# Eight of eleven up-projection iterations as seven block products of half-length matmuls, in a float32 decoder trunk on one Trainium2 core

## The reference, cut to what matters

```python
D_FF = ((8 * D_MODEL // 3 + 127) // 128) * 128        # 2816
def conv_ffn(x, norm_g, w_up, conv_w, conv_b, w_down):
    h = rms_norm(x, norm_g)
    a, b = jnp.split(h @ w_up, 2, axis=-1)
    a = lax.conv_general_dilated(a, conv_w[:, None, :], window_strides=(1,),
                                 padding=[(CONV_WIDTH - 1, 0)], ...
                                 feature_group_count=D_FF) + conv_b
    return (jax.nn.silu(a) * b) @ w_down
```

## Time and profile before

| | |
|---|---|
| median of 3 runs | 1625.05 us (1625.04 to 1625.46) |
| profiled execution | span 1624.1 us, 0.95 us less than the median |
| PE busy | 1617.6 us |
| DVE, ACT, POOL busy | 971.4, 670.6, 109.9 us |
| granted TensorE clock | 1.00 over the whole span |
| DMA | 154.59 MB, mean 95 GB/s |

### The profile page before, as it was taken

The page is one execution under the profiler, slowest core; times in us unless marked ns, Lnnn a source line. Parts: engine busy times, 40 slices in busy tenths (PEclk is TensorE's granted clock), DMA queues, the critical chain, the costliest instruction groups (busy, mean ns, idle before and its releaser), DMA issues.

```text
span 1624.1 us, 19782 instructions
## 1 busy us (share of the span) xinstructions
PE 1617.6 (100%) x7482; PEld 1348.9 (83%) x7482; DVE 971.4 (60%) x1167; ACT 670.6 (41%) x807; POOL 109.9 (7%) x157
## 2 busy tenths in 40 slices
PE   9999999999999999999999999999999999999998
PEld 7888888888888888888888888888888888888887
DVE  7267875775666666533362778657756666556222
ACT  5244335532345445522233543345333554454213
POOL 4000000000310000002020000000004000000020
PEclk9999999999999999999999999999999999999999
DMA  5332222223232323323233322222233322232322
GB/s 189 104 117 78 78 78 91 79 68 101 91 99 95 97 97 92 102 92 102 91 116 96 112 78 78 78 91 76 77 94 99 96 93 101 91 103 90 111 91 91
DMA packets 44701, 154.59 MB, mean 95 GB/s; under 512 B 4960, under 2 KB 5472, under 8 KB 44640
## 3 DMA queue, kind: packets, MB, share of 16 engines
q1 hardware_dynamic: 42480, 148.86, 28.0%
q10 hardware_dynamic: 2160, 4.86, 1.1%
HBM read 149.50 MB, written 2.10 MB: 93 GB/s over the span
## 4 chain that ended last, share of the span: by engine, by line
PE 99%; DMA 0%; DVE 0%; ACT 0%; issue 0%; SPq 0%; DVEq 0%; ACTq 0%
PE ps L1045 30%; PE ps L1043 30%; PE ps L1044 30%; PE ps L1051 2%; PE ps L1050 2%; PE ps L1049 2%; PE ps L1172 1%; PE ps L1161 1%; PE ps L1139 1%; PE ps L1143 1%; PE ps L1295 0%; PE ps L1183 0%; DMA xs<-xt 0%; PE ps L1109 0%; PE ps L1180 0%; PE ps L1340 0%
## 5 line engine op out<-in xcount | busy, mean ns | idle before, releaser
L1043 PE MATMUL ps<-u_hi,w_hi 128*128 128x512 f32 x1344 | 525.5, 391 | 0.0
L682 DVE TENSOR_TENSOR w_lo<-w_raw,w_hi 128x1024 fp32r<-128x1024 f32 x274 | 350.6, 1289 | 291.8 <-ACT w_hi L431 287.7
L1045 PE MATMUL ps<-u_hi,w_lo 128*128 128x512 f32 x1344 | 523.3, 389 | 0.0
L1044 PE MATMUL ps<-u_lo,w_hi 128*128 128x512 f32 x1344 | 523.2, 389 | 0.0
L431 ACT ACTIVATE w_hi<-w_raw 128x1024 fp32r<-128x1024 f32 x274 | 286.6, 1055 | 278.7 <-DMA w_raw<-wts 272.0
L1045 PEld LDWEIGHTS ps<-u_hi,w_lo 128*128 128x128 f32 x1344 | 252.3, 188 | 53.0
L1044 PEld LDWEIGHTS ps<-u_lo,w_hi 128*128 128x128 f32 x1344 | 252.5, 188 | 50.9
L1043 PEld LDWEIGHTS ps<-u_hi,w_hi 128*128 128x128 f32 x1344 | 252.5, 188 | 50.5
L1045 PE MATMUL ps<-g_hi,w_lo 128*128 128x512 f32 x264 | 102.7, 389 | 0.0
L1043 PE MATMUL ps<-g_hi,w_hi 128*128 128x512 f32 x264 | 102.7, 389 | 0.0
L1044 PE MATMUL ps<-g_lo,w_hi 128*128 128x512 f32 x264 | 102.7, 389 | 0.0
(11 more groups left out here) (211 smaller groups left out, 2190.1 us busy)
## 6 DMA issues: line engine op xcount, KB each, us to landing
w_raw<-wts SPq DMA_DIRECT2D x274, 512.0 KB, 3.5
q<-q ACTq DMA_DIRECT2D x8, 256.0 KB, 3.5
xs<-xt SPq DMA_DIRECT2D x7, 256.0 KB, 6.6
out<-rows SPq DMA_DIRECT2D x7, 256.0 KB, 2.5
dec<-decay ACTq DMA_DIRECT2D x2, 514.0 KB, 4.1
w_raw<-wts SPq DMA_DIRECT2D x4, 256.0 KB, 6.2
cs<-rope ACTq DMA_DIRECT2D x2, 512.0 KB, 3.6
lastg<-last ACTq DMA_DIRECT2D x1, 256.0 KB, 4.3
```

The costliest lines, as they stand in the source:

```text
L682: nc.vector.tensor_tensor(w_lo[:, s, :], w_raw[:, s, :], w_hi[:, s, :].bitcast(F32), ALU.subtract).then_inc(s_lo, 1)
L1043: nc.tensor.matmul(dst, a_hi, b_hi, start=start, stop=False)
L1044: nc.tensor.matmul(dst, a_hi, b_lo, start=False, stop=False)
L1045: return nc.tensor.matmul(dst, a_lo, b_hi, start=False, stop=stop)
```

## The change

Of the 11 up iterations of a layer the first three (`PLAIN`) stay as they are. The other eight (`SPLIT`) treat an iteration, which is a product of 512 x 1024 by 1024 x 512, as a 2 x 2 block product: tokens in an early and a late half, k in two halves, output channels in the `a` and the `b` half. Its four weight quarters are W11, W21 (both k halves of `a`), W12, W22 (of `b`). Eight block products would make it in the plain way; here seven are made, over sums of quarters and sums of activation blocks, and the four output blocks are put together from them.

* **Weights.** Seven parts of 128 x 1024 for each iteration: part 0 = W11, 1 = W11 + W12, 2 = W22 + part 1, 3 = W21, 4 = W12 + W22, 5 = W22, 6 = W21 + part 2. SP loads seven quarters (`load_split`). The second summand of parts 1 and 4 comes in by a DMA that POOL issues and that adds to what lies there (`add_parts`); parts 2 and 6 are added up by DVE (`third_sum`, `fourth_sum`). Then ACT and DVE split each part (`part_high`, `part_low`).
* **Activations**, once a layer: ACT applies the norm's gain (`with_gain`), POOL multiplies four and adds four blocks of 128 x 1024 (`combine`), and ACT and DVE split the seven results (`comb_high`, `comb_low`), the first three after the second plain iteration, the other four after the third.
* **PE.** A product has 2 x 4 x 3 = 24 matmuls of 128 x 256. Three banks are used. Products are accumulated on one another, and ACT copies intermediate sums out between them (`copy_x`, `copy_y`, `copy_u`), for which PE waits.
* **Outputs.** DVE makes three of the four blocks (2 x 256 per partition) from PSUM and a copy, ACT the last one. The convolution of iteration n runs during iteration n + 1; the gate product of a split iteration moves to POOL (`gated`) and stays unsplit in `g_raw`.
* **Down.** The seven activation sums lie where `g_hi` is to be. So the split of the gated tiles (`gated_high`, `gated_low`, two tiles at a time) is moved behind the products: pair 0 in the last split iteration, pair s + 1 during down slab s, on each engine behind the split of weight slab s + 3.

```diff
-DOWN0 = UP0 + 2 * FT
+PLAIN = 3
+PAIRS = FT // 2
+SPLIT = PAIRS - PLAIN
+DOWN0 = UP0 + 4 * PLAIN
...
+            def load_split(l):
+
+                base = l * SLABS + DOWN0 - RING + SLOT_CREDIT
+                sp.wait_ge(s_free, base + 1)
+                load_part(l, 0, 0, W11, s_el[0])
+                sp.wait_ge(s_free, base + 2)
+                load_part(l, 0, 1, W11, s_el[1])
+                sp.wait_ge(s_free, base + 3)
+                load_part(l, 0, 2, W22, s_el[2])
+                load_part(l, 0, 6, W21, s_el6[0])
+                sp.wait_ge(s_free, base + 4)
+                load_part(l, 0, 3, W21, s_el[3])
+                load_part(l, 0, 4, W12, s_el[4])
+                load_part(l, 0, 5, W22, s_el[5])
+                for n in range(SPLIT):
+                    done = 7 * (l * SPLIT + n)
+                    more = n + 1 < SPLIT
+                    if more:
+                        if n > 0:
+                            sp.wait_ge(s_prod, done)
+                        load_part(l, n + 1, 6, W21, s_el6[(n + 1) % 2])
+                    sp.wait_ge(s_prod, done + 1)
+                    if more:
+                        load_part(l, n + 1, 0, W11, s_el[0])
+                    else:
+                        load(ring(l, 0), l * SLABS + DOWN0)
...
+            def combine(l):
...
+                nc.gpsimd.tensor_tensor(a22[:], a22[:], late, ALU.mult).then_inc(s_v, 1)
+                nc.gpsimd.tensor_tensor(late2[:], late2[:], late, ALU.mult).then_inc(s_v, 1)
...
+            def add_parts(l, n, k):
+
+                landed, added, which = (s_el[1], s_sum1, W12) if k == 1 else (s_el[4], s_sum3, W22)
+                pool.wait_ge(landed, 16 * (l * SPLIT + n + 1))
+                nc.gpsimd.dma_start(part_raw(l, n, k), wts[DEPTH * SLABS + (l * SPLIT + n) * 4 + which, :, :],
+                                    accum_op=ALU.add).then_inc(added, 16)
...
+            def gated_high(l, c):
+
+                act.wait_ge(s_gf, l * FT + 2 * c + 2)
+                last = 7 * SPLIT * (l + 1)
+                act.wait_ge(s_prod, last - 6 if c < 2 else last)
+                nc.scalar.activation(g_hi[:, 2 * c:2 * c + 2, :], g_raw[:, 2 * c:2 * c + 2, :], ACT.Copy).then_inc(s_ghh, 1)
...
+                    if g == PLAIN - 1:
+                        for k in range(3, 7):
+                            comb_high(l, k)
+                for n in range(SPLIT):
...
+                    part_high(l, n, 3)
+                    act.wait_ge(s_prod, done + 1)
+                    if n > 0:
+                        act.wait_ge(s_c11, l * SPLIT + n)
+                    nc.scalar.activation(copy_x[:], half_tiles(banks(n)[0]), ACT.Copy).then_inc(s_cpx, 1)
+                    part_high(l, n, 4)
...
+                    act.wait_ge(s_prod, done + 2)
...
+                    nc.scalar.activation(copy_u[:], half_tiles(banks(n)[0]), ACT.Copy).then_inc(s_cpu, 1)
+                    part_high(l, n, 6)
+                    for k in range(3):
...
+                        else:
+                            split_hi(l, DOWN0 + k)
+                            if k == 1:
+                                gated_high(l, 0)
...
                 for i in range(DOWN0, SLABS):
...
                     if i + AHEAD < SLABS:
                         split_hi(l, i + AHEAD)
+                    if i - DOWN0 + 1 < PAIRS:
+                        gated_high(l, i - DOWN0 + 1)
...
+            def third_sum(l, n):
+
+                m = l * SPLIT + n
+                dve.wait_ge(s_sum1, 16 * (m + 1))
+                dve.wait_ge(s_el[2], 16 * (m + 1))
+                nc.vector.tensor_tensor(part_raw(l, n, 2), part_raw(l, n, 2), part_raw(l, n, 1), ALU.add).then_inc(s_sum2, 1)
+
+            def fourth_sum(l, n):
+
+                m = l * SPLIT + n
+                dve.wait_ge(s_sum2, m + 1)
+                dve.wait_ge(s_el6[n % 2], 16 * (l * (SPLIT // 2) + n // 2 + 1))
...
+            def gated_low(l, c):
+
+                dve.wait_ge(s_ghh, l * PAIRS + c + 1)
+                nc.vector.tensor_tensor(g_lo[:, 2 * c:2 * c + 2, :], g_raw[:, 2 * c:2 * c + 2, :], g_hi[:, 2 * c:2 * c + 2, :].bitcast(F32),
+                                        ALU.subtract).then_inc(s_gl, 2)
...
+                        elif i + AHEAD == DOWN0 + 2:
+                            third_sum(l, 0)
+                            fourth_sum(l, 0)
+                            part_low(l, 0, 1)
...
+                    dve.wait_ge(s_prod, 7 * m + 5)
+                    dve.wait_ge(s_cpy, m + 1)
+                    dve.wait_ge(s_gf, l * FT + 2 * (PLAIN + n))
+                    nc.vector.tensor_tensor(cb[:, :, S // 2:S], half_tiles(a), copy_y[:], ALU.subtract).then_inc(s_c22, 1)
+                    if n + 1 < SPLIT:
+                        third_sum(l, n + 1)
+                    else:
+                        split_lo(l, DOWN0 + 1)
+                        gated_low(l, 0)
+                    dve.wait_ge(s_prod, 7 * m + 6)
+                    dve.wait_ge(s_cpu, m + 1)
+                    nc.vector.tensor_tensor(cb[:, :, 0:S // 2], copy_u[:], half_tiles(c), ALU.subtract).then_inc(s_tile, 4)
+                    if n + 1 < SPLIT:
...
                     if i + AHEAD < SLABS:
                         split_lo(l, i + AHEAD)
+                    if i - DOWN0 + 1 < PAIRS:
+                        gated_low(l, i - DOWN0 + 1)
...
+                def product(n, k, bank, fresh, ends):
+
+                    hi, lo = part_hi(l, k), part_lo(l, n, k)
+                    pe.wait_ge(s_elo, 7 * (l * SPLIT + n) + k + 1)
+                    if n == 0:
+                        pe.wait_ge(s_combl, l * 7 + k + 1)
+                    for t in range(2):
+                        for kk in range(4):
+                            o = kk * 256 + t * P
+                            mm = three_open(ps[:, bank, t * 256:t * 256 + 256], hi[:, o:o + P], lo[:, o:o + P],
+                                            comb_hi[k][:, kk, :], comb_lo[k][:, kk, :], fresh and t == 0 and kk == 0, ends and kk == 3)
+                    mm.then_inc(s_prod, 1)
...
+                    product(n, 0, a, True, False)
+                    product(n, 1, c, True, False)
+                    pe.wait_ge(s_cpx, m + 1)
+                    product(n, 2, a, False, False)
+                    product(n, 3, b, True, True)
+                    pe.wait_ge(s_cpu, m + 1)
+                    product(n, 4, a, False, False)
+                    pe.wait_ge(s_cpy, m + 1)
+                    product(n, 5, c, False, True)
+                    pe.wait_ge(s_c22, m + 1)
+                    product(n, 6, a, False, True)
 
```

More of the change, by code:

```diff
@@ L305, in trunk @@
         s_gl = sem("s_gl")
+        s_v = sem("s_v")
+        s_xgain = sem("s_xgain")
+        s_comb = sem("s_comb")
+        s_combh = sem("s_combh")
+        s_combl = sem("s_combl")
+        s_el = [sem(f"s_el{k}") for k in range(6)]
+        s_el6 = [sem(f"s_el6{b}") for b in range(2)]
+        s_sum1 = sem("s_sum1")
+        s_sum3 = sem("s_sum3")
+        s_sum2 = sem("s_sum2")
+        s_sum4 = sem("s_sum4")
+        s_eh = sem("s_eh")
+        s_elo = sem("s_elo")
+        s_prod = sem("s_prod")
+        s_cpx = sem("s_cpx")
+        s_cpy = sem("s_cpy")
+        s_cpu = sem("s_cpu")
+        s_c11 = sem("s_c11")
+        s_c21 = sem("s_c21")
+        s_c22 = sem("s_c22")
+        s_ghh = sem("s_ghh")
         s_xga = sem("s_xga")
@@ L347, in _, with load_one, load_ring @@
             assert DEPTH * SLABS % RING == 0
-            with sp.Fori(1, DEPTH * SLABS // RING) as r:
-                for j in range(RING):
-                    sp.wait_ge(s_free, r * RING + j + 1)
-                    load(j, r * RING + j)
+            def load_one(n):
+                sp.wait_ge(s_free, n + 1)
+                load(n % RING, n)
+            def load_ring(first, end):
+                a, b = -(-first // RING), end // RING
+                for n in range(first, a * RING):
+                    load_one(n)
+                with sp.Fori(a, b) as r:
+                    for j in range(RING):
+                        sp.wait_ge(s_free, r * RING + j + 1)
+                        load(j, r * RING + j)
+                for n in range(b * RING, end):
+                    load_one(n)
@@ new lines, in plain_tap, with silu @@
+            def plain_tap(l, g, h):
+                f = 2 * g + h
+                act.wait_ge(s_tile, l * TILES + TILE_CREDIT + UP_TILE + 2 * f + 1)
+                if f >= 2:
+                    act.wait_ge(s_gf, l * FT + f - 1)
+                nc.scalar.activation(cc[:, h, :], ca[:, h, 2:2 + S], ACT.Identity, scale=taps(l, f, 2), bias=taps(l, f, 3)).then_inc(s_c1, 1)
+            def silu(l, f):
+                act.wait_ge(s_cv, l * 2 * FT + 2 * f + 2)
+                nc.scalar.activation(cc[:, f % 2, :], cc[:, f % 2, :], ACT.Silu).then_inc(s_c2, 1)
@@ L609, in _ @@
                 root(l, 1)
[L610 removed]
+                for g in range(PLAIN):
                     for j in range(4):
```

(22 more changed lines are left out.)

344 lines of the change are left out of this document (290 added, 54 removed).

## The result

The changed kernel takes **1650.46 us** (median of 4 runs, 1648.33 to 1652.25) against 1625.05 us for the kernel before (4 runs, 1624.83 to 1625.46). The ratio is 1.0155, 95% interval 1.0141 to 1.0169: 25.4 us slower. The profiled execution has a span of 1650.4 us, 26.3 more than the 1624.1 of before.

What follows compares the result with a forecast made beforehand. PE's matmul pace was taken to bound the kernel (busy 1617.6 of 1624.1 us). Pace -26.9, way in +9 and down-projection +25 made +7: span 1631, 1632 us with 0.95 outside it; own range 1628 to 1638, whole range 1615 to 1655.

Steps and rivals of the forecast that it cites:

- steady split iteration: Split iterations after each layer's first: every part split 2 us or more ahead of its product, no waits, 0 us.
- cover of part 4: Split iterations: 8.7 us from the start of part 4's accumulating DMA until its sum is needed; the DMA taken as 6.
- way in: First split iteration of each layer: PE waits 3.9 us before the third product, plus 0.6 for a DMA; +9 us.
- POOL's combine: POOL's eight blocks for the activation sums, about 3.2 us each, ending some 15 us before the first product; put at nothing.
- pace: Split iterations: 168 short matmuls at 0.1195 us take 20.08 us instead of 21.76; -26.9 us over 16 iterations.
- down-projection: PE waits 2.05 us at six down slabs a layer for the gated split standing behind a weight split; +25 us.
- short matmuls cannot be fed: Rival, split iterations: 168 short matmuls in a row run 0.005 us slower each, 13 us in all, 1645 us; chance 0.05.
- half the distance: Rival, split iterations: long runs of short matmuls go 0.1133 us apart, iteration 19.04 us, 1615 us in all; chance 0.08.
- In time for product 1: Each layer's first split iteration: low part 1 ready at 2.4 us after the last plain slab, before the second product.
- nothing, were all four low parts made earlier: Lower bound for each layer's first split iteration: no loss if the four activation low parts were made earlier.
- the tighter one: Split iterations: of the two accumulating DMAs, part 4's was held to have the less slack, 8.7 us.
- the sums by DMA are late: Rival: accumulating DMAs hold PE in each split iteration once they take over 8.7 us; 1665 us at 10.5; chance 0.15.

Runs made afterwards that it cites:

- down_first: Changed kernel with the gated split placed ahead of the weight split on ACT and DVE in the down-projection; 1626.60 us, ratio 1.0009 to the kernel before.
- entry_order: Changed kernel with DVE's low parts of activation sums 3 to 6 placed among the weights' low parts in each layer's first split iteration; 1655.38 us, ratio 1.0187.
- entry_dve_sum: Changed kernel with low parts of activation and weights interleaved in each layer's first split iteration, and part 4 summed there by DVE; 1644.14 us, ratio 1.0112.
- rebuilt2: Like rebuilt, but activation sums 3 to 6 are split within the last plain iteration; 1622.77 us, ratio 0.9988 to the kernel before.
- no_dma_sums: Changed kernel without its 32 accumulating DMAs, parts 1 and 4 left as single quarters, for timing only; 1643.52 us, ratio 1.0116.
- clock_probe: Kernel before, with PE made to wait at six slabs of the first down-projection for chains of one to six DVE products; 1659.44 us, ratio 1.0209.
- rebuilt3: Like rebuilt2, but part 1 too is summed by DVE, leaving no accumulating DMA; 1621.71 us, ratio 0.9985 to the kernel before.
- dve_sum: Changed kernel with part 4 summed by DVE instead of an accumulating DMA, part 1 keeping its DMA; 1645.04 us, ratio 1.0125.
- rebuilt: Changed kernel with the edits of down_first, entry_order and dve_sum together; 1622.77 us, ratio 0.9982 to the kernel before.
- first four variants: Changed kernel with, singly: gated split first, 1626.60 us; entry low parts interleaved, 1655.38; low part 1 ahead of `fourth_sum`, 1653.54; no accumulating DMAs, 1643.52.

## Why the forecast was wrong, step by step

The direction was right, the size was not: +7 us in the forecast, +25 to 26 measured, and 1650.5 lies far outside 1628 to 1638. The failed steps are these: the steady split iteration was put at nothing on the cover of part 4 alone (+6.5 measured), the way in was followed only up to the third product (+15.4 for +9), and the sum has no term for the clock behind a wait (about 10 of the 26.3 us, in the way in and the down stretches together). A smaller one is POOL's combine, put at nothing (+1.8 with all else). The term of the pace and the waits of the down-projection held.

- **The pace** was right: -27.5 for -26.9. The rivals "short matmuls cannot be fed" and "half the distance" are both out, by 20.04 us an iteration.
- **The down-projection** was right in mechanism, places and waits: 23.6 us of waits for 24.6 (6 x 2.05 x 2), at the six slabs named. down_first shows the cause. The term measured 30.1: 4.9 us more are matmuls at the lower clock behind three of the twelve waits, and 1.5 are small losses of some 0.1 us a slab.
- **The way in** (+9) measured 15.4. The wait ahead of the third product measured 3.95 for 3.9, in part by luck: low part 2 ended at T + 11.2 and not at 9.6, but the second product had been held back as well. Two things were not right. "In time for product 1" failed by 1.54 and 0.97 us: in layer 0 the quarter for `third_sum` took 5.9 us to land, beside the load of `w_odd` and the first accumulating DMA, and was there at T + 0.6 and not at T - 1.6. And I followed DVE's queue only up to that product. entry_order and entry_dve_sum show that a wait of 3.7 us for the accumulating DMA of part 4 and one of 3.1 us for DVE's combinations lay under it, so that the bound "nothing, were all four low parts made earlier" was false; rebuilt2 makes them earlier, and its way in is no shorter.
- **The steady split iteration** (0) measured 6.5. I priced the cover of part 4 at 8.7 us as "the tighter one" and did not price part 1's. From the trace: sum issued at 556.03, product due at 568.51, and 4.15 us from landing to product, so 8.3 us of cover. The typical sum took 6.9 us (I took 6), but they ran from 5.3 to 9.6. Five sums of part 1 took more than 8.3, and just the five products behind them waited for low part 1. A cover has to be held against the longest landing. no_dma_sums shows the cause, and the rival "the sums by DMA are late" was a part of the truth.
- **POOL's combine "at nothing"** cost 1.0 us a layer, PE's wait at one slab. Beside its work two weight splits took 6.80 us where the earlier trace rows have 2.36. The eight products and sums took 2.4 to 3.4 us each, near the 3.2 that I took; the cover of three slabs did not hold, and DVE's other work beside POOL was slowed as well (a gate product 2.1 us and not 0.7). This is read from the trace; no run without the combine was made. DVE and POOL of the changed kernel:

```profile
484.52 6.80 DVE L1007 TENSOR_TENSOR w_lo<-w_raw,w_hi 128x1024 fp32r<-128x1024 f32 x2
...
486.93 3.31 POOL L576 TENSOR_TENSOR comb<-comb,late 128x1024 f32<-128x1024 f32 x1
```

- **The cost that was missing** is the clock: some 9.9 us, 5.0 behind the waits on the way in and 4.9 in the down stretches. The kernel before had no waits of that length, so its trace had no row for it; an unknown that I should have bounded. clock_probe shows that a wait alone brings it.

What stays open: why executions of the changed kernel and its variants spread over 4 to 9 us, rebuilt3 without accumulating DMAs too (1620.9 to 1625.4), where the kernel before stays within 1.2. The clock is a part of it: rebuilt3's two runs over 1625 have a mean granted clock of 0.994, its six under 1622 have 0.997 or 0.998. In dve_sum and rebuilt time and clock do not go together like this. Open is also how little work DVE would need on the way in for the gain of the pace to come through; no version with less work there was tried.

## What to carry to other kernels

When a change gives PE new waits, price each twice: its length, and the slower matmuls behind it, which here followed most waits of 2.0 us and more. Where you take one wait away, follow all engines to the end of that stretch first, since here three waits of 3 to 4 us lay over one another, and entry_order, which took away the first, gave nothing by itself. Work that waits for a landing should stand behind work that doesn't: one swap of two lines was worth 24 us, nearly all of the loss.

## What the runs showed of the hardware

- **A long wait of PE costs more than itself.** In the five traces of the changed kernel and its first four variants, the lower level of the clock began behind none of 36 waits of 1.2 to 1.9 us, unless a longer one came first; the matmuls of the 9 us behind them lost 1.1 us at most, and 0.3 or less as a rule. Of 27 waits of 2.0 us and more, 19 were followed by a loss of 1.5 to 2.7 us at the lower level of the clock, and 8 (2.0 to 3.4 us long) by none. So a wait of that length makes it likely, not certain; what decides between the two I can't tell from these rows.
- **An accumulating DMA of 512 KB** from memory into SBUF, issued by POOL, took 5.3 to 9.6 us from issue to landing (median 6.9) with the DMA engines 76% busy over layer 0's split iterations, 3.26 us of all 16 engines against 1.63 for a plain load, and 0.86 us of POOL's queue.
- **DVE beside POOL**: a subtraction of 128x1024 took 3.4 us beside POOL's combine and not 1.2. By the Trainium skill (SBUF — State Buffer, SBUF: two separate sides) a VectorE operation with two SBUF inputs and a GpSimd operation that reads SBUF shut one another out for a whole instruction; the trace agrees, with two splits that took 6.80 us together beside POOL operations of 2.84 to 3.43.
